# First four x tiles turned in fp32 with LayerNorm gains applied by ScalarE, attention units ranked between the gate blocks, and the planner's transfer prices set per queue

## The reference

```
x    = LayerNorm_in(x)
u    = x @ W_in                    -> q 512 | k 128 | v 128 | GLU 1024 | gates 2048
y_a  = windowed attention(q,k,v)   (8 heads, 2 kv heads, +-128 tokens, bias, sink) @ W_attn_out
y_c  = silu(LayerNorm(depthwise conv31(GLU(u)))) @ W_conv_out
mix  = (sigmoid(g_a) * y_a + sigmoid(g_c) * y_c) @ W_out
h    = LayerNorm1(alpha * x + mix)
out  = LayerNorm2(alpha * h + (silu(h @ W_gate) * (h @ W_up)) @ W_down)     hidden width 2816
```

## Time and profile before

| | us |
|---|---|
| median of 3 runs | 896.11 |
| lowest, highest | 895.93, 1026.02 |
| the profiled execution | 896.54 |
| its slowest core's span (core 3) | 895.0 |
| spans of the other cores | 891.0 to 893.7 |
| mean granted TensorE clock of the cores | 0.995 to 0.999 |

### The profile page before, as it was taken

The page is one execution under the profiler, slowest core; times in us unless marked ns, Lnnn a source line. Parts: engine busy times, 40 slices in busy tenths (PEclk is TensorE's granted clock), DMA queues, the critical chain, the costliest instruction groups (busy, mean ns, idle before and its releaser), DMA issues.

```text
span 895.0 us, 14079 instructions; the slowest of 8 cores (891.0 to 895.0 us)
## 1 busy us (share of the span) xinstructions
PE 857.2 (96%) x4746; PEld 411.2 (46%) x4746; DVE 501.0 (56%) x791; ACT 244.6 (27%) x381; POOL 205.5 (23%) x291
## 2 busy tenths in 40 slices
PE   3899999899999999999999999999999999999996
PEld 1345557544444444444444444444444444444443
DVE  5899366686878887787874121236551212123565
ACT  1233355762636453433222111100001111110000
POOL 4245003133031320523343331112112111100121
PEclk9999999999999999999999999999999999999999
DMA  9786667485231423638799998525446555510321
GB/s 210 171 187 111 149 142 139 75 166 166 76 114 72 142 94 126 151 141 219 180 233 223 165 168 132 78 62 152 142 141 94 73 83 79 73 24 9 129 75 71
DMA packets 56487, 112.65 MB, mean 126 GB/s; under 512 B 21377, under 2 KB 21505, under 8 KB 56033
## 3 DMA queue, kind: packets, MB, share of 16 engines
q0 software_dynamic: 21600, 41.72, 31.3%
q1 hardware_dynamic: 34818, 70.03, 24.3%
HBM read 124.09 MB, written 27.26 MB: 169 GB/s over the span
## 4 chain that ended last, share of the span: by engine, by line
PE 88%; DVE 3%; issue 3%; DMA 3%; ACT 1%; POOL 1%; SPq 0%; POOLq 0%; DVEq 0%; ACTq 0%
PE ps L960 33%; PE ps L582 21%; PE ps L991 17%; PE ps L911 4%; PE ps L870 3%; PE ps L879 3%; PE ps L777 1%; PE ps L698 1%; DMA h_rows<-xr 1%; DMA lnrow<-lnp 1%; PE ps L810 1%; PE ps L748 1%; PE ps L549 1%; PE ps L647 1%; PE ps L532 1%
## 5 line engine op out<-in xcount | busy, mean ns | idle before, releaser
L968 DVE TENSOR_TENSOR hid<-ps,sgb 128x512 bf16<-128x512 f32 x88 | 60.8, 691 | 211.1 <-PE ps L960 207.1
L960 PE MATMUL ps<-hT,wEa 128*128 128x512 bf16 x704 | 154.6, 379 | 0.9 <-DMA xr<-x_rows 0.9
L960 PE MATMUL ps<-hT,wEb 128*128 128x512 bf16 x704 | 154.7, 379 | 0.0
L991 PE MATMUL ps<-wdn,hid 128*128 128x512 bf16 (+1 forms) x726 | 152.3, 373 | 0.0
L966 ACT ACTIVATE sgb<-ps 128x512 f32<-128x512 f32 x88 | 52.7, 598 | 319.5 <-PE ps L960 316.4
L582 PE MATMUL ps<-x0T,wga 128*128 128x512 bf16 x512 | 118.7, 379 | 1.7 <-POOL mT L891 1.0
L991 PEld LDWEIGHTS ps<-wdn,hid 128*128 128x128 bf16 x726 | 71.1, 98 | 81.2
L960 PEld LDWEIGHTS ps<-hT,wEa 128*128 128x128 bf16 x704 | 68.8, 98 | 83.7 <-issue 1.4
L960 PEld LDWEIGHTS ps<-hT,wEb 128*128 128x128 bf16 x704 | 68.8, 98 | 82.9
L891 POOL TENSOR_TENSOR mT<-gab,gab 128x512 bf16<-128x512 f32 x32 | 49.7, 1566 | 121.6 <-DVE gab L885 78.0
L582 PEld LDWEIGHTS ps<-x0T,wga 128*128 128x128 bf16 x512 | 48.9, 98 | 60.3 <-issue 4.0
(11 more groups left out here) (106 smaller groups left out, 916.4 us busy)
## 6 DMA issues: line engine op xcount, KB each, us to landing
xa<-x SPq DMA_DIRECT2D x16, 512.0 KB, 8.2
xb<-x SPq DMA_DIRECT2D x16, 512.0 KB, 4.2
x_rows<-xb SPq DMA_DIRECT2D x16, 512.0 KB, 2.8
xr<-x_rows SPq DMA_DIRECT2D x16, 512.0 KB, 5.3
h_rows<-xr SPq DMA_DIRECT2D x16, 512.0 KB, 5.7
hr<-h_rows SPq DMA_DIRECT2D x16, 512.0 KB, 4.8
out<-hr SPq DMA_DIRECT2D x15, 512.0 KB, 2.6
wEa<-wg POOLq DMA_DIRECT2D x22, 256.0 KB, 4.9
```

What stands on the lines that cost most here:

```text
L960: ins = e.matmul(bank(B), w[:, kc, :], hTv[tc][:, kc, :], start=(kc == 0), stop=(kc == 7))
L968: sc.add("dve", C_DVE, lambda e, U=U, sg=sg, c2=c2: e.tensor_tensor(hid[ffc][:, c2 * 512:(c2 + 1) * 512], bank(U), sg[:, :], ALU.mult), re ...
L991: ins = e.matmul(bank(B)[:, 0:cb - ca], hid[k][:, c0:c0 + 128], wdn[k][:, ca:cb], start=(k == 0), stop=(k == NFF - 1))
```

## The change

- **Tiles 0 to 3** no longer go through `ln_in`. `ln_first` leaves gain and bias out: after the statistics one DVE tensor_scalar does (x - mean) * 1/std in fp32 in place. `turn_first` turns two tiles together, in fp32: a PSUM bank takes two 128-column blocks of both tiles, four transposes a bank, four banks for a pair. ScalarE reads each block's 256 columns with its gain and bias, which lie along the partitions now and come from two new parts of the `small` table, and writes `x0T`. Tiles 4 to 15 go the old way.
- **Order of loads at the start**: x tile 0, `lnrow`, `small`, x tile 1, `ident32`, x tiles 2 and 3. The first `wgl` pair waits for x tile 1, the later ones for the 1/std of the tile ahead. x tiles 4 to 7 wait for `wgl0` to `wgl3`. `ident`, `cbias` and the three bias tables are held back (behind tile 3's 1/std, x tile 12), `wqk` loads are let go sooner.
- **Ranks of attention**: units 0 to 3 from 301.1 to 164, unit n from 4 on from 400 to 397.95 + 10 * (n // 4), with 0.2 a unit: a unit now stands among the gate blocks of the token group before.
- **The planner's prices**: each queue is a server of its own, 0.31 MB/us, 2.0 us fixed on SP and 2.4 on POOL, and two that overlap slow each other; a cast load counts the fp32 bytes that it reads. "tr" may hold four banks. Some costs are changed: lnrow's products 1.8, POOL's sum 1.57, a product 0.214 for 512 columns, the transposing load 930.

```diff
@@ -24,7 +24,9 @@
 C_CONVLB = 20
 C_SINK = 24
 C_DELTA = 32
-C_SMALL = 40
+C_LNG = 40
+C_LNB = 48
+C_SMALL = 56
 
 
 class Bank:
@@ -68,8 +70,8 @@
     NBANK = 8
     HOP = 0.15
     SWITCH = 1.3
-    DMA_FIXED = 2.0
-    DMA_RATE = 0.19
+    DMA_FIXED = {"sp": 2.0, "pool": 2.4}
+    DMA_RATE = 0.31
 
     def __init__(self, caps, free_names):
         self.free_names = free_names
@@ -152,7 +154,7 @@
                 ready[op.eng].append(op)
         free = {e: 0.0 for e in self.ENGS}
         table = None
-        dma_free = 0.0
+        dma_free = {"sp": 0.0, "pool": 0.0}
         dma_hist = {e: [] for e in self.ENGS}
         bank_prev = [[] for _ in range(self.NBANK)]
         bank_at = [0.0] * self.NBANK
@@ -209,9 +211,14 @@
             if op.dma:
                 issue = 0.53 if e == "pool" else 0.45
                 free[e] = st + issue
-                t0 = max(st + self.DMA_FIXED, dma_free)
-                dma_free = t0 + op.cost / 1024.0 / self.DMA_RATE * 1.0
-                op.fin = dma_free
+                other = "sp" if e == "pool" else "pool"
+                t0 = max(st + self.DMA_FIXED[e], dma_free[e])
+                work = op.cost / 1024.0 / self.DMA_RATE
+                both = max(0.0, min(work, 0.5 * (dma_free[other] - t0)))
+                op.fin = t0 + work + both
+                dma_free[e] = op.fin
+                if both > 0.0:
+                    dma_free[other] += both
                 dma_hist[e].append(op.fin)
             else:
                 c = op.cost
@@ -323,7 +330,7 @@
     x0_d = nc.dram_tensor("x0_rows", [S, D], F32, kind="Internal").ap()
     h_d = nc.dram_tensor("h_rows", [S, D], F32, kind="Internal").ap()
 
-    sc = Sched(dict(tr=2, proj=3, sc=4, o=2, y=2, mix=2, gu=6, dn=4, cv=2),
+    sc = Sched(dict(tr=4, proj=3, sc=4, o=2, y=2, mix=2, gu=6, dn=4, cv=2),
                ("xl", "slot", "glu_d", "h_d", "x0_d", "out_d", "gu"))
 
     def sb(off, shape, dt, name):
@@ -477,7 +484,7 @@
 
 
     def c_mm(n, cols=512):
-        return n * (0.004 + 0.213 * cols / 512.0)
+        return n * (0.004 + 0.214 * cols / 512.0)
 
     C_ACT = 0.6
     C_ACT1K = 1.05
@@ -486,7 +493,7 @@
     C_STAT = 1.36
 
     def cast_load(kb, dst_ap, src_ap, writes, reads=()):
-        sc.dma("pool", kb, lambda e: e.dma_start(out=dst_ap, in_=src_ap), reads=reads, writes=writes)
+        sc.dma("pool", 2 * kb, lambda e: e.dma_start(out=dst_ap, in_=src_ap), reads=reads, writes=writes)
 
     def load(kb, dst_ap, src_ap, writes, reads=(), transpose=False):
         if transpose:
@@ -540,25 +547,57 @@
 
     sc.prio = 0
     sc.add("dve", 0.1, lambda e: e.memset(negh[:, :], -0.5), writes=["negh"])
-    for t in range(4):
+    load(512, xa[0][:, :], x_d[0:128, :], ["xa0", ("xl", 0)])
+    load(8, lnrow[0:1, :], lnp_d[0:1, 0:2 * D], ["lnrow"])
+    load(28, small[:, :], small_d, ["small"])
+    load(512, xa[1][:, :], x_d[128:256, :], ["xa1", ("xl", 1)])
+    load(64, ident32[:, :], ident_d, ["ident32"])
+    for t in range(2, 4):
         load(512, xa[t][:, :], x_d[t * 128:(t + 1) * 128, :], ["xa%d" % t, ("xl", t)])
-    load(8, lnrow[0:1, :], lnp_d[0:1, 0:2 * D], ["lnrow"])
     sc.add("dve", 0.1, lambda e: e.memset(onesr[0:1, :], 1.0), writes=["onesr"])
     for k in range(4):
         B = Bank("proj")
-        sc.add("pe", 0.9, lambda e, k=k, B=B: e.matmul(bank(B), onesr[0:1, :], lnrow[0:1, k * 512:(k + 1) * 512],
-                                                       start=True, stop=True), reads=["onesr", "lnrow"], writes=[B])
+        sc.add("pe", 1.8, lambda e, k=k, B=B: e.matmul(
+            bank(B), onesr[0:1, :], lnrow[0:1, k * 512:(k + 1) * 512], start=True, stop=True),
+            reads=["onesr", "lnrow"], writes=[B])
         sc.add("act", C_ACT, lambda e, k=k, B=B: e.copy(lnin[:, k * 512:(k + 1) * 512], bank(B)),
                reads=[B], writes=[("lnin", k // 2)])
-    cast_load(32, ident[:, :], ident_d, ["ident"])
-    load(20, small[:, :], small_d, ["small"])
-
+
+
+    def ln_first(t):
+        xs, xn = xa[t], "xa%d" % t
+        stats(xs, xn, mvX[:, 2 * t:2 * t + 2], ("mvX", t))
+        inv_std(rsX[:, t:t + 1], mvX[:, 2 * t + 1:2 * t + 2], EPS, 1, [("mvX", t)], [("rsX", t)])
+        sc.add("dve", 0.8, lambda e: e.tensor_scalar(
+            xs[:, :], xs[:, :], mvX[:, 2 * t:2 * t + 1], rsX[:, t:t + 1], ALU.subtract, ALU.mult),
+            reads=[xn, ("mvX", t), ("rsX", t)], writes=[xn])
+
+    def turn_first(t0):
+        for h in range(4):
+            B = Bank("tr")
+            for t in (t0, t0 + 1):
+                xs, xn = xa[t], "xa%d" % t
+
+                def f_tr(e, h=h, B=B, t=t, xs=xs):
+                    ins = None
+                    for i in range(2):
+                        kc = 2 * h + i
+                        c0 = i * 256 + (t - t0) * 128
+                        ins = e.transpose(bank(B)[:, c0:c0 + 128], xs[:, kc * 128:(kc + 1) * 128], ident32[:, :])
+                    return ins
+                sc.add("pe", 2 * 0.24, f_tr, reads=[xn, "ident32"], writes=[B])
+            for i in range(2):
+                kc = 2 * h + i
+                sc.add("act", 0.42, lambda e, i=i, kc=kc, B=B: e.activation(
+                    x0Tv[0][:, kc, t0 * 128:(t0 + 2) * 128], bank(B)[:, i * 256:(i + 1) * 256], AF.Identity,
+                    bias=small[:, C_LNB + kc:C_LNB + kc + 1], scale=small[:, C_LNG + kc:C_LNG + kc + 1]),
+                    reads=[B, "small"], writes=[("x0T0", t0), ("x0T0", t0 + 1)])
 
     def ln_in(t):
         i = t % 5
         xs, xn = xa[i], "xa%d" % i
-        if t >= 4:
-            load(512, xs[:, :], x_d[t * 128:(t + 1) * 128, :], [xn, ("xl", t)])
+        load(512, xs[:, :], x_d[t * 128:(t + 1) * 128, :], [xn, ("xl", t)],
+             reads=["wgl%d" % (t - 4)] if t < 8 else [])
         stats(xs, xn, mvX[:, 2 * t:2 * t + 2], ("mvX", t))
         inv_std(rsX[:, t:t + 1], mvX[:, 2 * t + 1:2 * t + 2], EPS, 1, [("mvX", t)], [("rsX", t)])
         sc.add("dve", C_DVE1K, lambda e: e.scalar_tensor_tensor(
@@ -600,20 +639,25 @@
     for tc in range(4):
         sc.prio = 100 + 10 * tc
         for i in range(4):
-            ln_in(4 * tc + i)
-            if tc == 0:
-                for k in (4 + i, i):
-                    cast_load(256, wgl[k][:, :], win_d[6 + k], ["wgl%d" % k], reads=[("xl", i)])
+            if tc:
+                ln_in(4 * tc + i)
+                continue
+            for k in (4 + i, i):
+                cast_load(256, wgl[k][:, :], win_d[6 + k], ["wgl%d" % k], reads=[("rsX", i - 1) if i else ("xl", 1)])
+            ln_first(i)
+            if i % 2:
+                turn_first(i - 1)
+        if tc == 0:
+            cast_load(32, ident[:, :], ident_d, ["ident"], reads=[("rsX", 3)])
         sc.prio = 105 + 10 * tc
         for cc in range(4):
             glu_block(tc, cc)
     sc.prio = 130
     for k in range(6):
-        cast_load(256, wqk[k][:, :], win_d[k], ["wqk%d" % k], reads=[("xl", 6 + k)])
+        cast_load(256, wqk[k][:, :], win_d[k], ["wqk%d" % k], reads=[("xl", 5 + k // 3)])
     sc.prio = 131
     cast_load(768, taps[:, :], taps_d, ["taps"], reads=[("xl", 12)])
-    load(64, ident32[:, :], ident_d, ["ident32"])
-    load(192, cbias[0:96, :], convb_d[0:96, :], ["cbias"])
+    load(192, cbias[0:96, :], convb_d[0:96, :], ["cbias"], reads=[("xl", 12)])
     sc.prio = 135
     sc.add("pool", 3.0, lambda e: e.memset(vones[:, :], 1.0), writes=[("vones", i) for i in range(4)])
     sc.add("dve", 0.1, lambda e: e.tensor_scalar(hbias[:, :], small[:, C_BGATE:C_BGATE + 16], 0.5, None, ALU.mult),
@@ -759,7 +803,7 @@
     sc.prio = 140
     for j in range(3):
         sc.prio = 122
-        load(512, biast[j][:, :], bias_d[j], ["biast%d" % j])
+        load(512, biast[j][:, :], bias_d[j], ["biast%d" % j], reads=[("xl", 12)])
     pctr = [0]
 
     def att_front(n):
@@ -838,7 +882,7 @@
 
     def att_units(us):
         for n in us:
-            sc.prio = (400 + (n // 4) * 10 if n >= 4 else 301.1) + (n % 4) * 0.2
+            sc.prio = (397.95 + (n // 4) * 10 + (n % 4) * 0.2) if n >= 4 else 164 + (n % 4) * 0.2
             for k in range(n, min(n + 2, 16)):
                 if k not in fr and k // 4 == n // 4:
                     fr[k] = att_front(k)
@@ -888,7 +932,7 @@
         sc.add("dve", C_DVE, lambda e: e.scalar_tensor_tensor(
             gv, gv, 1.0, bank(Yc).rearrange("p (r i) -> p i r", r=16), ALU.add, ALU.mult),
             reads=[gcn, Yc], writes=[gcn])
-        sc.add("pool", 1.27, lambda e: e.tensor_tensor(mTv[tc][:, f, :], ga[:, :], gc[:, :], ALU.add),
+        sc.add("pool", 1.57, lambda e: e.tensor_tensor(mTv[tc][:, f, :], ga[:, :], gc[:, :], ALU.add),
                reads=[gan, gcn], writes=["mT%d" % tc] + [("slot", (2 * k + w) % NG) for w in range(2)])
 
     def gates(tc):
@@ -930,7 +974,7 @@
     def turn_late(t, after):
         tc, i = t // 4, t % 4
         hb, hn = (hbl if t < 12 else hbk)[t % 4], "%s%d" % ("hbl" if t < 12 else "hbk", t % 4)
```

(4 more changed lines are left out.)

## The result

The changed kernel takes 1.0055 times the time of the kernel before, 95% interval 1.0033 to 1.0077: about 901 us. Forecast were 884.5 us and a range up to 895, so both sign and range missed. In two of its four executions one die ran at a lower clock; the ratio leaves them out. The profiled execution took 899.33 us, span 897.4, against 896.54 and 895.0.

A forecast was written before the change was run, and what follows sets the result against it. TensorE was taken as the bound, busy 857.2 of 895.0 us, its idle time winnable only ahead of 425 us. 6.2 + 1.3 + 2.0 + 2.5 = 12.0 us off 896.54 gave 884.5; range 876 to 895.

The forecast's parts named there:

- a rival that ended at 890 to 895: Only the start pays; new prices miss single loads in contention, so projections wait and mixing only moves stalls; chance 0.18.
- an aside of 0 to 3 us at tile 7: Before block two: if new prices put it right behind block one, a late tile 7 costs 0 to 3 us.
- the prices for matmul cost nothing by themselves: In the planner: the changed matmul prices, listed with moved bias tables and tr banks, were taken to cost nothing.
- the 4.5 forecast as won: Attention ranks: 2.0 us won in the Silu stretch and 2.5 from mixing units with gate blocks.
- The first projection: Start of the kernel: first projection at about 23.2 instead of 29.46, 6.2 us won, between 4 and 8.
- only the last two: End of the start's path: ScalarE activations run under the next bank's transposes, so only two show, 0.9 with hops 0.2.
- Slow projections: Block one, behind the first transposes: the 2.2 us of slow projections stay and only move.
- Tile 7: Before block two: tiles 4 to 7 arrive between about 22 and 33, so tile 7's lateness of 1.3 us is won.
- Silu stretch: 165 to 178 us: q, k, v projections left for the Silus fill TensorE; 2.0 of 3.4 us idle won.
- Attention mixing: 191 to 425 us: mixing units 4 to 15 with gate blocks wins 2.5 us; bounds 6 won, 4 lost.
- The rival in which attention units stall TensorE: Gate blocks: 12 mixed units each cost a 1.0 us wait, giving 901; slower than before had chance 0.11.
- whatever is won ahead of it reaches the end: Ahead of 425 us: the feed-forward half is full and only shifts, so earlier gains reach the end.

The follow-up runs named there:

- s_wqk: e_start with the wqk loads let go at x tiles 6 to 11 again, as in the kernel before; 0.9989 of the kernel before.
- a_pad: The changed kernel with the xb loads in x0_rows and xr loads in mix priced at twice their bytes, in the plan only; 0.9960 of the kernel before.
- e_start: The new start alone (first four tiles, order and gates of loads, four tr banks) with old prices and old ranks; 0.9936 of the kernel before.
- e_prices: The kernel before with all the planner's new prices alone; 1.0126 of the kernel before, 11.3 us slower.

## Why the prediction was wrong, by its own steps

**The step that failed** is a term that isn't in the sum. The transfer prices went into it at nothing, without a reason, and came up only in a rival that ended at 890 to 895 and in an aside of 0 to 3 us at tile 7. What the prediction does say, that "the prices for matmul cost nothing by themselves", held: the compute prices alone gave 0.9984. Measured, the transfer prices cost 11.1 us on the kernel before, and the set of all prices 12.8 on the new start and 5.8 where the new ranks are in as well.

They aren't the whole miss. The changed kernel came out 16.7 us above the forecast, and the kernel with start, ranks and old prices (0.9990, 895.4 us) still lies 10.9 above it. Taken in the order start, ranks, prices, the start fell short by 1.8 us (5.7 for the 6.2 and 1.3 forecast), the ranks by 9.3 (4.8 lost for the 4.5 forecast as won) and the prices by 5.8. In the order start, prices, ranks it is 1.8, 12.8 and 2.3. The parts don't add, and which of them is named the largest depends on that order. Either way the sign of the result is the prices': with old ones the kernel is level with the one before or a little faster (0.9990, up to 1.0000), with two pads faster (0.9960). The rival had the mechanism (prices "met by the total rate of rows 7 but not by single loads in contention") but wrong place and size: it named tiles and weights of the start, while the transfers that cost are the second reading of x in `x0_rows`, that of x0 in `mix`, and the stores ahead of both, 165 to 425. A rate made from the earlier trace rows is true for the total and says nothing of a single transfer. The price of 3.6 us lies even under the medians of 4.0 and 5.0; a pass placed by it in a list that is executed in order is late more often than not, and everything behind it on the DVE is late too.

**The first projection**: forecast 23.2, came at 24.03, inside 4 to 8 us won. Four terms were off and nearly cancelled, so the number is close by luck. The lnrow row landed at 5.85 ("near 6"), and its products ended at 13.0. But tiles 0 and 1 weren't turned right behind them: the TensorE waited 1.9 us, to 14.87, for tile 0's tensor_scalar, which the DVE has in its list behind the statistics of all four tiles. `tensor_scalar` took less than my doubled 1.08: by form, in 10 to 60 (busy us, mean ns)
```profile
L591 ACT ACTIVATE x0T<-ps,small 128x256 bf16<-128x256 f32 x16 | 7.4, 599 | 2.8 <-PE ps L586 2.8
...
L571 DVE TENSOR_SCALAR xa<-xa,mvX,rsX 128x1024 f32<-128x1024 f32 x4 | 3.1, 806 | 1.1 <-POOL rsX L522 1.0
```
0.8 us, which the estimate from the Trainium skill (VectorE: DVE Perf Modes, Mode 2×_2P) had said and I hadn't taken. Sixteen fp32 transposes took 3.0 (32 in 5.93), not 4.4. And the end of the path isn't "only the last two" activations: ScalarE turns out 256 columns every 0.46 us, 16 need 7.40 in a row from 16.49 on, and TensorE, done at 20.8, waits 3.2 for them. So ScalarE bounds the new start. The Trainium skill (ScalarE: Activation LUTs, What ACT_TABLE_LOAD costs) has an operation's time rise with its columns on top of a fixed part of 186 ns, plus 93 for each operand from a pointer, and lets neighbours overlap by 93: 0.49 us for one of 256 columns here, an estimate from that page, near the measured 0.46. That alone wouldn't have shown the bound beforehand: a bank needs two activations, 0.92 us as measured, and its four transposes were forecast at 1.1. They took 0.74, and so the ScalarE became the slower of the two.

**Slow projections.** Forecast: the 2.2 us of slow projections move along. They did, and grew: block one took 16.6 us. Stretches of the changed kernel from 21 on, and behind them the first 4 us of block one in the kernel before:
```profile
21.00:24.00 3.00, 0.00 (x0) 0.00 (x0) 0.00 (x0) 2.89 (x7) 0.00 (x0) 0.82 1.08 238
24.00:28.00 4.00, 3.97 (x10) 1.50 (x11) 1.75 (x4) 0.30 (x1) 0.22 (x1) 0.50 1.02 226
28.00:30.00 2.00, 2.00 (x7) 0.71 (x5) 1.34 (x2) 0.30 (x1) 1.36 (x2) 0.56 1.06 234
30.00:32.00 2.00, 2.00 (x11) 0.88 (x9) 2.00 (x3) 0.00 (x0) 1.68 (x3) 1.00 1.01 304
```
```profile
29.40:33.40 4.00, 3.94 (x10) 1.45 (x11) 3.29 (x4) 0.27 (x1) 1.89 (x2) 1.00 0.92 309
```
The engine idles from 20.8 to 24.0, the granted clock falls to 0.50 (1.2 GHz), and ten products need 4 us where eleven need 2.0 at 1.00 (2.4 GHz). Before, ten took as long with a reading of 1.00: the reading doesn't show every slow stretch. The Trainium skill's rule (TensorE: Matmul & The Clock Gate, Part 4) that transposes don't count as activity agrees as far as the fall comes behind 32 of them; the idle time between would explain it as well, and no run here separates the two.

**Tile 7**: forecast a landing by 33 and 1.3 us won; it landed at 43.4, and tile 6's transposes, held behind it, waited 1.8. The count of bytes left out six wqk loads that tiles 5 and 6 release in that very window, and it took tile 7's load to leave when its own gate opens, though its place in SyncE's list is behind tiles 8 and 9. The diff shows the wqk loads, and *s_wqk* puts their price at 1.8 us at block two (3.6 less the moved products).

**Silu stretch**: forecast 2.0 won, was 3.0. The step gave this to the ranks; but ranks alone left 1.5 us idle there at a granted clock of 0.82 (0.93 before), and the transfer prices alone left 0.8 at 1.00. So more than the ranks fills it. **Attention mixing**: forecast 2.5 won, bounds 6 won to 4 lost. 191 to 425 came out 12.5 us idle against 6.7, of which *a_pad* shows most to be the prices of the xb and xr loads (4.3 idle there). For the ranks themselves the comparisons give +2.2 to −4.8 us: within the bounds, with a sign that changes with the plan around it. The rival in which attention units stall TensorE for ScalarE and DVE didn't come: no wait repeats once a unit.

**What the sum assumed**: that "whatever is won ahead of it reaches the end". For one fixed order that is so. But this kernel's order is written anew for each edit, and then 3.6 us more at block two went with 4.7 us less at the end. *e_start* reached 5.7 us; how much of that is its start and how much a lucky order isn't settled. The other kernels with the new start and old or padded prices end between 0.9958 and 0.9990.

## What to carry to other kernels

Price a load in a planner for in-order queues at what it takes when things go badly, at least where other work stands behind its user: a rate made true to the total took at least 1 us of slack off each load, turned it into waits and cost 11 us, although no instruction changed. Price the store that frees a buffer in the same way: the load behind it can't leave before it has landed, and at the worst place it took twice as long as the load. Split such a change into parts before trusting its sum, and where an edit makes a new plan, hold the orders fixed and change the load (or the cost) itself, so that the wait and the luck of the order come apart. Don't judge an early stage by when the next one starts if a planner may move work across that border; compare idle time. In a chain that is to be shortened, multiply each engine's smallest repeated step by its count: the last steps show alone only if the engine keeps up.

## What the hardware showed that was not expected

- The granted clock can read at half speed through a stretch that is fully busy: 3.97 of 4.0 us, ten products of 512 columns. In *a_pad* 5.6 us of waiting behind tile 7's load did the same later on: sixteen products took 5.58 us at 49.62 where sixteen of the same take 3.62 at 39.63. So these two waits of the TensorE, of 3.2 and 5.6 us, were each followed by some 2 us more; the one of 1.8 us at 46.96 was followed by sixteen at 3.62.
- A 512 KB load of xb or xr takes 4 to 5 us from issue to landing in the median; those of x between 10 and 60 us take 8.5 in the median and up to 11.8. A 512 KB store to `x_rows` takes 3.0 us in the median, but single stores took 8.2 us (337 us into the changed kernel) and 10.3 (*e_prices*, beside four 512 KB cast loads). Six 256 KB cast loads took 11.0 in the median between 10 and 60 us, where the 16 engines were full.
- fp32 transposes of 128x128 run at 0.185 us each at the start, against 0.15 in the dense stretch of the earlier trace rows, though seven microseconds of one-row products and a wait of 1.9 lie ahead of them.
